# Moving four query tiles of a projection into the stage that turns and compresses key and value rows

## What is computed

```
n  = mod(norm(x))
qa, kva, ga, ... = split(n @ w_in[l])            # 512 query columns, 768 key/value columns, 24 gates, ...
sub = kv[:, :n_sub * 16].reshape(B, n_sub, 16, NSA_GROUPS, NSA_DH)
h = b1 + sum over r in (0, 1) of einsum('bnjgd,jde->bnge', sub[:, r:r + n_cmp], w1[r])
compressed = einsum('bnge,ed->bngd', silu(h), w2) + b2
```

## Time and profile before

| what | us |
|---|---|
| median of three runs | 3393.26 |
| the profiled execution, as a run | 3394.81 |
| its span in the profile | 3393.0 |
| PE busy in it | 3085.4 (91%) |
| DVE busy, ACT busy | 1357.9, 964.5 |
| projection, first to last product, layer 0 | 523.5 to 595.0 |
| rows stage, first row turn to end of compression, layer 0 | 601.1 to 675.8 |
| layer 1, the same two | 2173.9 to 2246.2, 2252.2 to 2327.8 |

### The profile page before, as it was taken

How to read it: one execution, slowest core, us unless ns; L and a number is a source line. 1 busy time by engine, 2 the same in 40 slices (tenths; PEclk the granted TensorE clock), 3 DMA queues, 4 the chain that set the end, 5 groups by cost and what they waited for, 6 DMA issues and landing times. The chain is left out here.

```text
span 3393.0 us, 58789 instructions
## 1 busy us (share of the span) xinstructions
PE 3085.4 (91%) x24907; PEld 2919.5 (86%) x24907; DVE 1357.9 (40%) x2813; ACT 964.5 (28%) x1594; POOL 55.4 (2%) x32
## 2 busy tenths in 40 slices
PE   6999998699679998999989999878987899899997
PEld 4999998578469998999989999867865898899997
DVE  4232344256236354333342333433541735533334
ACT  2222222244133143222232222322430513322222
POOL 0000000000011000000000000000000300000000
PEclk7999998799769898999999999889986889899998
DMA  6645334232333245333256422443122525233321
GB/s 216 227 155 171 89 83 146 71 112 57 106 100 86 79 136 174 121 89 88 80 173 202 150 88 85 129 126 99 54 57 69 142 63 156 69 88 88 88 88 64
DMA packets 523702, 378.64 MB, mean 112 GB/s; under 512 B 43058, under 2 KB 469448, under 8 KB 522131
## 3 DMA queue, kind: packets, MB, share of 16 engines
q1 hardware_dynamic: 486932, 307.17, 30.9%
q10 hardware_dynamic: 36512, 67.77, 5.7%
HBM read 344.10 MB, written 39.07 MB: 113 GB/s over the span
## 5 line engine op out<-in xcount | busy, mean ns | idle before, releaser
L192 DVE TENSOR_TENSOR w_lo<-w_raw,w_hi 128x1024 fp32r<-128x1024 f32 (+1 forms) x390 | 481.3, 1234 | 1125.8 <-ACT w_hi L187 1125.7
L187 ACT ACTIVATE w_hi<-w_raw 128x1024 fp32r<-128x1024 f32 (+1 forms) x390 | 405.7, 1041 | 1333.6 <-PE pa L204 680.9
L204 PE MATMUL pa<-nhi,w_hi 128*128 128x272 f32 x1408 | 296.7, 292 | 29.1 <-DVE nlo L247 27.3
L204 PE MATMUL pa<-nhi,w_lo 128*128 128x272 f32 x1408 | 293.2, 290 | 0.0
L204 PE MATMUL pg<-nhi,w_hi 128*128 128x272 f32 x1408 | 292.9, 289 | 0.0
L204 PE MATMUL pa<-ghi,w_hi 128*128 128x272 f32 x1408 | 291.6, 288 | 1.3 <-DVE glo L794 1.3
L204 PE MATMUL pg<-nhi,w_lo 128*128 128x272 f32 x1408 | 292.5, 289 | 0.0
L204 PE MATMUL pa<-nlo,w_hi 128*128 128x272 f32 x1408 | 292.4, 289 | 0.0
L204 PE MATMUL pg<-nlo,w_hi 128*128 128x272 f32 x1408 | 291.9, 289 | 0.0
L204 PE MATMUL pa<-ghi,w_lo 128*128 128x272 f32 x1408 | 291.0, 288 | 0.0
L204 PE MATMUL pa<-glo,w_hi 128*128 128x272 f32 x1408 | 290.4, 288 | 0.0
(11 more groups left out here) (340 smaller groups left out, 4750.7 us busy)
## 6 DMA issues: line engine op xcount, KB each, us to landing
w_raw<-in_ffn_w_in SPq DMA_DIRECT2D x352, 192.0 KB, 2.8
ada_raw<-in_ada_w ACTq DMA_DIRECT2D x26, 2048.0 KB, 10.0
w_raw<-in_w_in SPq DMA_DIRECT2D x156, 192.0 KB, 2.9
w_raw<-in_ffn_w_out SPq DMA_DIRECT2D x128, 192.0 KB, 2.7
w_raw<-in_ffn_w_in SPq DMA_DIRECT2D x176, 128.0 KB, 2.9
ada_raw<-in_ada_w SPq DMA_DIRECT2D x10, 2048.0 KB, 15.6
w_raw<-in_ffn_w_out SPq DMA_DIRECT2D x160, 128.0 KB, 2.4
w_raw<-in_w_in SPq DMA_DIRECT2D x94, 128.0 KB, 3.1
```

Source lines behind the costliest of these rows:

```text
L187: act.activation(self.hi[slot][:, 0:k, :], self.raw[slot][:, 0:k, :], ACT.Copy).then_inc(self.hi_done, 1)
L192: dve.tensor_tensor(self.lo[slot][:, 0:k, :], self.raw[slot][:, 0:k, :], self.hi[slot][:, 0:k, :].bitcast(F32), ALU.subtract).then_inc(sel ...
L204: mm = pe.matmul(out[:, half, 0:HALF], w[slot][:, k0 + n, :], x[:, n, half * HALF:(half + 1) * HALF], start=(n == 0 and w is self.hi and x ...
```

## The change

The list of projection tiles is cut in two: keys, values and gates stay in the projection (7 tiles), the 4 query tiles go to the rows stage, whose own first two are loaded and split in the projection; the attention's first two are now loaded and split in the rows stage. There PE does half a query tile (24 matmuls) behind the turn of each cached sequence, 8 halves for 4 tiles, into `pq`, which is one of the two buffers that `po` had. The copies of the row turns on ACT now use the two banks of the other one. Copies and splits of a query tile stand behind the gather of every second sequence on DVE and ACT. The DMAs of the compression weights move from ACT's queue to SP's, where they are followed by the load of tile 2; tiles 3 to 5 are loaded behind the cache rows of sequences 4 to 6. PE's second output product waits until the last query tile is copied out, since both use `po[1]`. The running index of tiles counts 7 and 4 instead of 11.

```diff
-            return [query(r) for r in range(R)] + [wt.columns(DC, w[:, C_KV + n * P:C_KV + (n + 1) * P]) for n in range(NKV)] \
-                + [wt.columns(DC, w[:, C_GATE:C_GATE + P])]
+            return [wt.columns(DC, w[:, C_KV + n * P:C_KV + (n + 1) * P]) for n in range(NKV)] \
+                + [wt.columns(DC, w[:, C_GATE:C_GATE + P])], [query(r) for r in range(R)]
...
-                tiles = proj_tiles(l) + follow
-                NT = R + NKV + 1
+                tiles = proj_tiles(l)[0] + follow
+                NT = NKV + 1
...
-                        chunk = (Q0 + t) if t < R else (KV0 + t - R) if t < R + NKV else GATE0
-                        dve.tensor_scalar(pj[:, chunk, :].rearrange("p (h t) -> p h t", h=2), pp[t % 2][:, :, 0:HALF],
-                                          DH ** -0.5 if t < R else 1.0, None, ALU.mult).then_inc(ev_done, 1)
+                        chunk = KV0 + t if t < NKV else GATE0
+                        dve.tensor_copy(pj[:, chunk, :].rearrange("p (h t) -> p h t", h=2), pp[t % 2][:, :, 0:HALF]).then_inc(ev_done, 1)
...
+                pa = ph
+                pb = [po[0][:, i:i + 1, :] for i in range(2)]
+                pq = po[1]
+                tiles = proj_tiles(l)[1] + follow
...
                     sp.wait_ge(sig_done, 1)
                     sp.dma_start(gate_dram.rearrange("b g i -> g b i"), pj[0:3 * HEADS, GATE0, SEQ:T].rearrange("g (b i) -> g b i", i=NI)).then_inc(gate_out, 16)
+                    for kv in range(2):
+                        for j in range(2):
+                            sp.dma_start(w1[kv][j * DH:(j + 1) * DH, :, :, :],
+                                         a["cmp_w1"][l, kv, :, j::2].rearrange("r m d e -> d r m e")).then_inc(w_in, 16)
+                        sp.dma_start(w2[:, kv, :], a["cmp_w2"][l, kv]).then_inc(w_in, 16)
+                    wt.load(sp, wt.at(2), tiles[2])
                     for b in range(4, NB):
                         sp.wait_ge(tr_done, 2 * (b - 3))
                         load_rows(sp, l, b, cn, rows_in[b % 4])
+                        if b < R + 3:
+                            wt.load(sp, wt.at(b - 1), tiles[b - 1])
...
                             ins.then_inc(done, 1)
+                        if s < NB and s % 2:
+                            between(s // 2)
...
+                        i, second = divmod(b, 2)
+                        u, slot = wt.at(i)
+                        if not second:
+                            pe.wait_ge(wt.lo_done, 2 * u + slot + 3)
+                            if i >= 1:
+                                pe.wait_ge(ev_done, i)
+                        mm = wt.some(pe, slot, pq, nhi, nlo, DC, 4 * second, 4 * second + 4)
+                        if second:
+                            mm.then_inc(wt.mm_done, 1)
...
+                        if q == 1:
+                            pe.wait_ge(ev_done, R)
...
+                    def query(i):
+                        wt.multiplied(dve, wt.at(i))
+                        dve.tensor_scalar(pj[:, Q0 + i, :].rearrange("p (h t) -> p h t", h=2), pq[:, :, 0:HALF],
+                                          DH ** -0.5, None, ALU.mult).then_inc(ev_done, 1)
+                        wt.split_lo(dve, wt.at(i + 2), DC)
+
+                    gather(dve, 1, cb_done, query)
...
-                    for kv in range(2):
-                        for j in range(2):
-                            act.dma_start(w1[kv][j * DH:(j + 1) * DH, :, :, :],
-                                          a["cmp_w1"][l, kv, :, j::2].rearrange("r m d e -> d r m e")).then_inc(w_in, 16)
-                        act.dma_start(w2[:, kv, :], a["cmp_w2"][l, kv]).then_inc(w_in, 16)
...
-                    gather(act, 0, ca_done)
+                    gather(act, 0, ca_done, lambda i: wt.split_hi(act, wt.at(i + 2), DC))
...
-                    proj_stage(l, pj, cn, nhi, nlo, attention_tiles(l)[0:2])
+                    proj_stage(l, pj, cn, nhi, nlo, proj_tiles(l)[1][0:2])
...
+                        rows_stage(l, pj, kvn, gn, kct, vcn, cn, oa, ob, nhi, nlo, attention_tiles(l)[0:2])
```

More of the change, by code:

```diff
@@ L968, in load_rows, with rows_stage @@
                     "o p k g d -> (o p) k (g d)")).then_inc(done, 16)
-        def rows_stage(l, pj, kvn, gn, kct, vcn, cn, oa, ob):
+        def rows_stage(l, pj, kvn, gn, kct, vcn, cn, oa, ob, nhi, nlo, follow):
             NM = CMP_STRIDE // 2
             with stage(nc, "sig_done", "rt_done", "va_done", "sc_done", "out_done", "gate_out", "rows0", "rows1", "rows2",
-                       "rows3", "w_in", "tr_done", "ca_done", "cb_done", "silu_done", "o_done", "oe_done", "x_done") as (
+                       "rows3", "w_in", "tr_done", "ca_done", "cb_done", "silu_done", "o_done", "oe_done", "x_done", "ev_done") as (
                     sig_done, rt_done, va_done, sc_done, out_done, gate_out, rows0, rows1, rows2, rows3, w_in, tr_done,
-                    ca_done, cb_done, silu_done, o_done, oe_done, x_done), ExitStack() as st:
+                    ca_done, cb_done, silu_done, o_done, oe_done, x_done, ev_done), ExitStack() as st:
                 rows_in = [rows0, rows1, rows2, rows3]
@@ L992, in rows_stage @@
                 po = [ps(f"po{i}", 2, st) for i in range(2)]
-                pa, pb = ph, po
+                pa = ph
+                pb = [po[0][:, i:i + 1, :] for i in range(2)]
+                pq = po[1]
+                tiles = proj_tiles(l)[1] + follow
                 block = st.enter_context(nc.Block())
@@ L1012, in _, with gather @@
                     sp.wait_ge(gate_out, 16)
-                def gather(engine, g, done):
+                def gather(engine, g, done, between):
                     rows = slice(g * DH, (g + 1) * DH)
@@ L1101, in _ @@
                         dve.tensor_copy(kvn[0:r, t, 0:512], pa[t % 2][0:r, 0, :]).then_inc(va_done, 1)
-                    gather(dve, 1, cb_done)
+                    def query(i):
[4 more added lines that the diff above has]
+                    gather(dve, 1, cb_done, query)
                     for q in range(4):
@@ L1138, in _ @@
                                        bias=vecs[:, bass.ds(56 + l * 2 + q // 2, 1)]).then_inc(silu_done, 1)
+                wt.base += R
         def load_sequence(sp, l, b, kv, done):
@@ L2094, in mixer @@
                         vcn = sb("vcn", [NCMP, NSEQ, P], at=nsa)
-                        rows_stage(l, pj, kvn, gn, kct, vcn, cn, oa, ob)
+                        rows_stage(l, pj, kvn, gn, kct, vcn, cn, oa, ob, nhi, nlo, attention_tiles(l)[0:2])
                         early.close()
@@ L2105, in trunk @@
         for l in range(DEPTH):
-            ffn_stage(l, 0, 0, proj_tiles(l)[0:2])
+            ffn_stage(l, 0, 0, proj_tiles(l)[0][0:2])
             mixer(l)
```

## The result

| | before | changed |
|---|---|---|
| median (lowest to highest), us | 3393.76 (3388.26 to 3395.55), 4 runs | 3356.53 (3353.11 to 3358.35), 4 runs |
| ratio, 95% interval | | 0.9892 [0.9875, 0.9909] |
| span of the profiled execution | 3393.0 | 3351.3 |

The page's busy line of the changed kernel answers to the earlier trace rows: PE does the same number of matmuls in 12 us less, since more of them run at the fast clock. (Fast or warm: a granted clock of 1.00 in the windows, that is 2.4 GHz; slow or cold: 0.50, 1.2 GHz.)

What follows compares the result with a forecast made beforehand. PE, busy 91% of the span, bounds the projection; in row and cache turns it idles almost half the time, waiting for ACT's issues, copies and DMA. Terms of -17.5 and -18.2 us took 3393.3 to 3358, range 3349 to 3374.

Steps and rivals of the forecast that it cites:

- Projection: Projection stage: four tiles fewer at 5.97 us each, -23.9 us a layer, or -21.6 if the narrow loads are late.
- ACT freed: Row turns: without six DMA issues on ACT, PE's third row tile waits 0.56 us; -3.6 us layer 0, -2.9 layer 1.
- Cache turns: Cache turns take eight half tiles: 36.1 us from first turn to compression, +11.2 us in layer 0, +9.8 in layer 1.
- Compression: Compression's first 64 matmuls start warm, 15.6 instead of 16.82 us: -1.2 us a layer.
- DVE's margin: Cache turns: DVE's gather ready 0.1 us before PE's odd turn; waits put at 0, bounds 0 and +0.5 us a pair.
- SP: Cache turns: SP issues a tile and four pages in 6.5 us; rows 7 out by 27.5, 2 to 3 us spare.
- The sum: Whole kernel: -17.5 us in layer 0 and -18.2 in layer 1, together -35.7.
- Loads late: Rival 1: SP's one queue delays rows 7 or the projection's end by 2 to 6 us a layer; 3362 to 3370; 0.14.
- Pairs stall on DVE: Rival 2, cache turns: 4.2 us copy, split, gather chain exposed; half gives 3375 us, all of it 3391; chance 0.08.
- Slower: Rival 3: PE's clock stays at 1.2 GHz in the cache turns, +23.5 us a layer, 3405 in all; chance 0.05.
- More: Rival 4, cache turns: half tiles at 3.0 us and a shorter first one; 3350 to 3353 us; chance 0.08.
- Nothing moves: Rival 5: queries' loads and PE's order give the time back elsewhere, as in attention's first tiles; 3390 us and above; 0.03.

Runs made afterwards that it cites:

- e1: The kernel before with one edit: SP instead of ACT issues the six compression-weight DMAs, behind the gate transfer; 3385.86 us, ratio 0.9974.
- e2: The changed kernel with the six compression-weight DMAs put back on ACT; 3362.71 us, ratio 0.9909.
- e7: The changed kernel with SP's order changed: query tiles 2 and 3 loaded first, attention's first two behind all cache rows and split behind the gathers; 3355.74 us.
- e5: The changed kernel itself, measured again; 3357.6 us, ratio 0.9897.
- e10: The changed kernel itself, measured once more; 3356.79 us, ratio 0.9893.
- e6: The changed kernel with query tiles loaded as 128 neighbouring columns, in 512-byte instead of 256-byte pieces (other queries computed); 3355.07 us, ratio 0.9895.
- e4: The changed kernel with 22 of the 24 matmuls of each half tile left out, so queries are not computed; 3357.03 us, ratio 0.9893.
- e3: The changed kernel with all eight half tiles behind the last cache turn instead of one behind each; 3400.96 us, ratio 1.0017.
- e8: The changed kernel with e7's order, tile 0 before the row turns, tile 1 between them, tiles 2 and 3 behind cache turns 3 to 6; 3360.44 us.
- e9: The changed kernel with e7's SP order, query tile 0 at the stage's head, tiles 1 to 3 in parts behind all eight cache turns; 3348.18 us, ratio 0.9868.

## Why the prediction was right

The mechanism was right term by term; one term was mis-sized, and that the forecast still lies within 1.5 us of the median is partly luck, as the sum below shows.

- **Projection, -23.9 a layer.** -23.9 in layer 0 and -24.0 in layer 1. In layer 0 the split of tile 8 waited for PE, as worked out, and the tile before it for DMA, 0.3 us late. In layer 1 four of five splits are put down to DMA. The prediction put landing at 2.9 to 3.4 us though the earlier trace rows has 4.3 for one issue; tile 7's slowest took 4.1.
- **ACT freed, -3.6 and -2.9.** Measured from the first row turn to the first cache turn: -3.6 and -2.9; e1 and e2 show it from both sides. The Trainium skill (DMA: Bandwidth & Descriptors, Issuing engines are not separate DMA queues) says that issuing from another engine only saves the sequencer's time, which is usually small relative to the DMA itself. The prediction made of this that the term would be near 0, which is more than the page says. What was saved is such time, 6.77 us of issuing on ACT, and it counted because the next instruction there was a copy that PE waited for.
- **Cache turns, +11.2 and +9.8.** +9.0 and +7.1: the term that was mis-sized, 4.9 us in the sum. I added durations of rows (1.1 for a turn, 3.2 for a half tile) in which the last matmul's tail lies over the next row's start. From start to start a warm turn is 0.78 and the half tile behind it 3.09, so a sequence is 3.87 and not 4.3. That is 7 x 0.43 = 3.0 us less in layer 0, of which three waits of 0.27 give 0.8 back: 2.2. In layer 1 the clock also rose 1 us sooner in the first half tile.
- **Compression, -1.2.** -1.5 and -1.6.
- **DVE's margin.** 0.1 to 0.2 us for the gather, as forecast; the copy, put in time by 0.3 us, was late by 0.14 since the turn ahead of it is short too. 0.25 us a pair, inside the bound of 0.5.
- **SP.** Rows 7 out 26.9 us after the first turn against 27.5. Four cache pages take 3.7 us and not 4.3; the row of 17.31 us that I divided by four holds waits for the turns. In layer 1 they had no time to spare rather than 2 to 3 us, mostly because PE asked for them some 2 us sooner than I had it. e7 shows that the order of SP's queue costs less than 1 us a layer.
- **The sum.** Stages from the norm to attention: 165.7 and 166.6 us before, 145.8 and 145.1 after, -41.4 against -35.7. The profiled executions differ by as much (3394.81 and 3353.11), the medians by 37.2. So the terms were 5.7 us too small for the executions whose stages can be seen, and the median moved by 4 us less than those: two errors that nearly cancel, which is luck. All three profiled executions of the changed kernel were the lowest of their four runs; why, and so what the other runs' stages look like, stays open.

**The rivals.** *Loads late* (1) happened in small. PE's idle time ahead of layer 1's row turns is 7.36 us in this execution, 7.15 in e5 and 6.03 in e10:

```profile
2177.26 1.06 ACT L187 ACTIVATE w_hi<-w_raw 128x1024 fp32r<-128x1024 f32 x1 [8.58 <-DMA w_raw<-in_w_in]
...
2201.24 1.06 ACT L187 ACTIVATE w_hi<-w_raw 128x1024 fp32r<-128x1024 f32 x1 [4.99 <-DMA w_raw<-in_w_in]
2207.17 1.11 PE L1052 MATMUL ph<-ident,pj 128*128 128x128 f32 x4 [7.36 <-ACT pj L1151]
...
2246.48 1.09 PE L1067 MATMUL pt<-ident,cn 128*128 128x128 f32 x8 [0.26 <-DMA cn<-in_cache_nsa_kv]
```

The stage's length from norm to sigmoid is 63.4 us all the same (63.5 in layer 0; 63.2 to 64.9 in the other kernels with the shorter list): PE was done 1.3 us sooner there, but the last split (2201.24) waits for its load, and the stage ends 3.9 us behind that split in both layers. *Pairs stall on DVE* (2) showed as 0.25 us. *Slower* (3) fell: the window of the cache turns has clock 0.93. *More* (4) was right in its cause, half tiles of 3.0, and its 3350 to 3353 is where the profiled execution ended, not the median. *Nothing moves* (5) fell with the total.

On the narrow query loads the Trainium skill (DMA: Bandwidth & Descriptors, Specifications) says that transfers under 512 B miss line rate. Had that doubled the time to landing, as the prediction supposed, the time would be 4.6 us higher. These runs show a cost, but a small one: the same load lands 0.5 to 0.6 us sooner in wide pieces (e6), the few tenths that the prediction read from the earlier trace rows, and the total is not measurably faster.

## What to carry to other kernels

Work of the tensor engine put between steps that wait for copies or transfers can be free (e4) or cost everything (e3). It has to stand behind every step, the first above all (e8 against e9). A product ahead of a run of short steps can pay by their clock alone (the row turns of e9). Filling such a stage shifts the bound: once filled, the queue that feeds it was nearly level with the engine, and less product no longer helped. And in a sum over pipelined matmuls, take differences of starts, not lengths of rows.

## What the runs showed of the hardware

- DMA issues are not alike. A cache page behind a page number read into a register took SP 0.92 us (3.68 for four), a part of a weight tile 0.5 (1.50 for three), and the same three 4.32 us right behind 2.1 MB of compression weights, of whose own issues one took up to 2.71. With pieces of 512 instead of 256 bytes the three took 2.35 there (e6).
- The five row tiles took 9.9 us at a granted clock of 0.50 in the changed kernel, with PE busy in 8.1 of them, behind 6.0 us of idle time; in e9, behind a product, 6.3 us at 1.00, with the same three pauses of 0.56 us.
- How long a pause is doesn't say by itself whether the clock falls. In e3 PE ran four transposes at the fast clock (0.63 us), was idle for 1.50 us, and the next turn ran at half speed (1.97 us), while in the kernel before a turn behind 1.59 us of idle time was fast (1.09 us, at 627.65). These runs don't show what decides.
- Tile 0 of e9, behind 4.1 us of idle time, started slow (six matmuls in 1.36 us, 0.75 when fast) and was fast after 6.0 us; layer 1's, behind 5.7 us, after 3.7.
